# Column sums, roots of three columns and a predicted sum for the renewed x in the norms of a diffusion trunk step

## What is computed

```
h = modulate(x, norm_pre[0], m0, m1);  y = swiglu(h, gate, up, down)
x = x + 0.5 * m2 * rmsnorm(y, norm_post[0])
h = modulate(x, norm_pre[1], m3, m4);  y = token_mixer(h)     # three mixers, then w_out
x = x + m5 * rmsnorm(y, norm_post[1])
h = modulate(x, norm_pre[2], m6, m7);  y = swiglu(h, ...)
x = x + 0.5 * m8 * rmsnorm(y, norm_post[2])
modulate(x, g, shift, scale) = rmsnorm(x, g) * (1 + scale) + shift,   rmsnorm(x, g) = x / sqrt(mean(x^2) + eps) * g
m0..m8 = silu(cond) @ ada_w + ada_b, one set for context, one for latent tokens
```

## Time and profile before

| | us |
|---|---|
| median of 3 runs | 2229.18 (2228.59 to 2231.0) |
| profiled execution, from first to last instruction | 2228.5 |
| PE busy in it | 2145.9 |
| DVE, ACT, POOL busy | 915.8, 903.4, 1240.8 |
| DMA | 311.37 MB, mean 140 GB/s |

### The profile page before, as it was taken

The page is one execution under the profiler, slowest core; times in us unless marked ns, Lnnn a source line. Parts: engine busy times, 40 slices in busy tenths (PEclk is TensorE's granted clock), DMA queues, the critical chain, the costliest instruction groups (busy, mean ns, idle before and its releaser), DMA issues.

```text
span 2228.5 us, 32128 instructions
## 1 busy us (share of the span) xinstructions
PE 2145.9 (96%) x13212; PEld 2022.6 (91%) x13212; DVE 915.8 (41%) x1486; ACT 903.4 (41%) x1269; POOL 1240.8 (56%) x972
## 2 busy tenths in 40 slices
PE   6999999999899999999999999999999899899998
PEld 4999997988898988999979999799888899799997
DVE  5122116446766465121251221534576664622122
ACT  3222323246765534223243232324567546432332
POOL 2666553444478464666646666354435955366663
PEclk8999999999999999999999999999999999899999
DMA  7555674433222384445554446552322235244431
GB/s 282 160 163 172 224 237 162 124 88 95 67 86 86 109 297 117 129 133 171 193 185 124 138 124 234 194 152 87 87 78 76 86 114 176 61 136 128 124 123 67
DMA packets 306921, 311.37 MB, mean 140 GB/s; under 512 B 9923, under 2 KB 285655, under 8 KB 306775
## 3 DMA queue, kind: packets, MB, share of 16 engines
q1 hardware_dynamic: 299671, 303.55, 43.4%
q10 hardware_dynamic: 7104, 5.77, 0.8%
HBM read 305.35 MB, written 3.93 MB: 139 GB/s over the span
## 4 chain that ended last, share of the span: by engine, by line
PE 73%; DVE 12%; ACT 8%; POOL 3%; issue 2%; DMA 1%; SPq 0%; DVEq 0%; ACTq 0%
PE X L588 56%; PE S L588 6%; PE Ab L588 4%; POOL w_lo L525 2%; PE S L705 1%; ACT w_hi L1028 1%; POOL dec L553 1%; POOL dec L552 1%; PE X L766 1%; PE S L795 1%; ACT p L1181 1%; DVE mg_lo L1453 1%; DVE gate_b L1464 1%; PE X L848 1%; DVE root L1560 1%
## 5 line engine op out<-in xcount | busy, mean ns | idle before, releaser
L525 POOL TENSOR_TENSOR w_lo<-raw,w_hi 128x512 fp32r<-128x512 f32 (+1 forms) x872 | 1163.6, 1356 | 947.2 <-ACT w_hi L1028 938.2
L1028 ACT ACTIVATE w_hi<-raw 128x1024 fp32r<-128x1024 f32 (+1 forms) x436 | 453.3, 1041 | 723.6 <-PE X L588 687.7
L588 PE MATMUL X<-h_hi,w_hi 128*128 128x384 f32 x1600 | 539.7, 337 | 12.6 <-DVE h_lo L1518 12.6
L588 PE MATMUL X<-h_lo,w_hi 128*128 128x384 f32 x1600 | 536.8, 335 | 0.0
L588 PE MATMUL X<-h_hi,w_lo 128*128 128x384 f32 x1600 | 536.6, 335 | 0.0
L588 PEld LDWEIGHTS X<-h_hi,w_hi 128*128 128x128 f32 x1600 | 302.0, 189 | 24.5 <-DVE h_lo L1518 15.9
L588 PEld LDWEIGHTS X<-h_lo,w_hi 128*128 128x128 f32 x1600 | 302.0, 189 | 0.0
L588 PEld LDWEIGHTS X<-h_hi,w_lo 128*128 128x128 f32 x1600 | 301.9, 189 | 0.0
L1590 DVE TENSOR_TENSOR prod<-X,silu 128x768 f32<-128x768 f32 x44 | 42.1, 957 | 566.7 <-PE X L588 566.7
L588 PE MATMUL X<-act_hi,w_hi 128*128 128x384 f32 x704 | 236.4, 336 | 0.0
L588 PE MATMUL X<-act_hi,w_lo 128*128 128x384 f32 x704 | 235.3, 334 | 0.0
(11 more groups left out here) (364 smaller groups left out, 3075.3 us busy)
## 6 DMA issues: line engine op xcount, KB each, us to landing
raw<-in_w_in SPq DMA_DIRECT2D x124, 512.0 KB, 3.8
raw<-in_ffn_gate SPq DMA_DIRECT2D x88, 512.0 KB, 3.8
raw<-in_ffn_up SPq DMA_DIRECT2D x88, 512.0 KB, 3.7
raw<-in_ffn_down SPq DMA_DIRECT2D x80, 512.0 KB, 3.5
raw<-in_ada_w SPq DMA_DIRECT2D x48, 512.0 KB, 3.9
hold<-in_ada_w SPq DMA_DIRECT2D x29, 512.0 KB, 5.2
first_w<-in_ada_w SPq DMA_DIRECT2D x16, 512.0 KB, 10.6
hold_a<-in_ada_w SPq DMA_DIRECT2D x16, 512.0 KB, 6.4
```

The costliest lines, as they stand in the source:

```text
L525: ins = nc.gpsimd.tensor_tensor(slot(w_lo, u)[:, part], raw_of(u)[:, part], slot(w_hi, u)[:, part], SUB)
L588: mm = nc.tensor.matmul(dst, w[:, k, m * 128:m * 128 + 128], r_, start=start and k + j == 0, stop=stop and k == u.nk - 1 and j == 2)
L1028: A(slot(w_hi, u), raw_of(u), ACT.Copy).then_inc(hi_ready[u.split], 1)
```

## The change

Sums over D are made by matmuls that have the tile of squares as the stationary operand and a column of `pick` (three columns wide, a single one filled) as the moving one (`token_sums`): the sum of token p of block b lands in partition p, column b of a 128x3 tile. ACT takes the root of the 128x3 tile (`r_q`), DVE its reciprocal (`r_t`), and `spread` brings it back to 128 x 384: the column, broadcast to 128 columns, is stationary and the identity moves. The result stays in PSUM (`SPREAD`, banks S6 and S5).

The sum of squares of the new x isn't made from x. With g = gate * y and r the reciprocal root of y, it is the old sum + 2r * sum(x*g) + r^2 * sum(g*g) (`x_sum`, `grown`; `grown` is kept from going below minus the old sum). For that DVE makes g tile by tile (`gated`), x*g (`with_x`), adds both kinds of squares (`added`), and ACT squares y and g, a tile at a time (`squared`, `gated_squared`). The last pair is taken in two halves: PE signals its first tile with `half_done`.

`post` and `pre` become `joint`: x is renewed a tile at a time between the small steps, and the last five tiles between the scaled tiles; `SPREAD[1]` is read by them from PSUM. S6 is no longer a bank of `MOD`, which has two now, and the take of the gap's first group moves into `joint`, behind the scaled tile of k = 3; it was behind all of `pre`. PE's ada units are split 2, 3 and the rest. ACT's last `highs` of a y phase moves from behind the squares of the last pair into `gap`. In an `out` phase the factors of the next norm are made at pair 0 instead of 3. `first_pre` uses the short sums, too; `last_post` gets its factor spread, and `r_tok` from `r_q` directly. POOL's loop keeps its order. `first_in` semaphores are merged into `loaded`.

```diff
-        MOD = [Ab, S7, S6]
+        MOD = [Ab, S7]
+        SPREAD = (S6[:, 0:T], S5[:, 0:T])
...
-                if u.first and g >= 3:
-                    pe.wait_ge(S["ada_copied"], g - 2)
+                if u.first and g >= 2:
+                    pe.wait_ge(S["ada_copied"], g - 1)
...
+            def token_sums(dst, rows, start, stop):
+                for b, r in enumerate(tokens(rows)):
+                    mm = nc.tensor.matmul(dst[:, 0:NB], r, pick[:, NB - 1 - b:2 * NB - 1 - b], start=start and b == 0,
+                                          stop=stop and b == NB - 1)
+                return mm
+            def spread(dst, col):
+                for b in range(NB):
+                    mm = nc.tensor.matmul(dst[:, b * 128:b * 128 + 128], col[:, b:b + 1].broadcast_to([128, 128]), ident,
+                                          start=True, stop=True)
+                mm.then_inc(S["spread_ready"], 1)
+            def y_sums():
+                pe.wait_ge(S["parts_ready"], seen.next("parts_ready"))
+                token_sums(S5, silu[:, 0, :], True, False)
+                pe.wait_ge(S["y_sq_ready"], seen.next("y_sq_ready", KT) - 1)
+                token_sums(S5, prod[:, 0, :], False, False)
+                pe.wait_ge(S["y_sq_ready"], seen.value("y_sq_ready"))
+                token_sums(S5, prod[:, 2, :], False, True).then_inc(S["sum_ready"], 1)
             def gap(units):
                 y_sums()
-                early = 12 if len(units) > 12 else len(units) // 2
-                for u in units[:early]:
+                for u in units[:2]:
                     ada_unit(u)
-                x_sums([])
-                for u in units[early:]:
+                pe.wait_ge(S["r_ready"], seen.next("r_ready"))
+                spread(SPREAD[0], r_t)
+                pe.wait_ge(x_free[0], seen.value(("xf", 0)) + 1)
+                pe.wait_ge(S["parts_ready"], seen.next("parts_ready"))
+                token_sums(X[0][:, 0, 0:NB], y_sum, True, False)
+                pe.wait_ge(S["c_made"], seen.next("c_made", KT) - 1)
+                token_sums(X[0][:, 1, 0:NB], silu[:, 1, :], True, False)
+                token_sums(X[0][:, 1, 0:NB], prod[:, 1, :], False, False)
+                pe.wait_ge(S["parts_ready"], seen.next("parts_ready"))
+                token_sums(X[0][:, 0, 0:NB], part, False, True)
+                pe.wait_ge(S["c_made"], seen.value("c_made"))
+                token_sums(X[0][:, 1, 0:NB], prod[:, 3, :], False, True).then_inc(S["cross_ready"], 1)
+                for u in units[2:5]:
+                    ada_unit(u)
+                pe.wait_ge(S["r_ready"], seen.next("r_ready"))
+                spread(SPREAD[1], r_t)
+                for u in units[5:]:
                     ada_unit(u)
                 return by_tiles
...
             def x_sums(units):
                 for k in range(KT):
                     pe.wait_ge(S["x_sq_ready"], seen.next("x_sq_ready"))
-                    mm = nc.tensor.matmul(S5[:, 0:T], ones, sq[:, k, :], start=k == 0, stop=k == KT - 1)
+                    mm = token_sums(S5, sq[:, k, :], k == 0, k == KT - 1)
                     if k % 2 and k // 2 < len(units):
                         ada_unit(units[k // 2])
                 mm.then_inc(S["sum_ready"], 1)
+                pe.wait_ge(S["r_ready"], seen.next("r_ready"))
...
-                            act.wait_ge(unit_done[u.split], u.split_turn + 1)
                             outputs[u.tag[0]](u)
-                        highs(u.n + SPLIT + 1)
+                        if u.tag != ("y", 3) or not u.last:
+                            highs(u.n + SPLIT + 1)
...
-            def gap(units):
-                root_of_sums()
-                act.wait_ge(S["ada_used"], units[2].n + 1)
-                x_squares(0, KT)
-                root_of_sums()
+            def root_of_sums(sums):
+                A(r_q[:, :], sums, ACT.Sqrt, bias=eps[:, 0:1], scale=1.0 / D).then_inc(S["root_ready"], 1)
+            def gap(units, upto):
+                highs(upto)
+                act.wait_ge(S["x_sum_made"], seen.next("x_sum_made"))
+                root_of_sums(x_sum[:, :])
                 act.wait_ge(S["ada_used"], units[:9][-1].n + 1)
                 h_highs(0, KT)
...
+            def y_squares(halves_done, cross):
+                def squared(u, k):
+                    if k >= 3:
+                        act.wait_ge(S["y_added"], seen.next("y_added"))
+                    A(prod[:, k % 2 * 2, :] if k else silu[:, 0, :], X[u.dest][:, k % 2, 0:T], ACT.Square).then_inc(S["y_sq_ready"], 1)
+                def gated_squared(k):
+                    act.wait_ge(S["g_made"], seen.next("g_made"))
+                    A(prod[:, k % 2 * 2 + 1, :] if k else silu[:, 1, :], y[:, k, :], ACT.Square).then_inc(S["c_made"], 1)
+                def go(u):
+                    i = u.tag[1]
+                    if i < 3:
+                        act.wait_ge(unit_done[u.split], u.split_turn + 1)
+                        for k in (2 * i, 2 * i + 1):
+                            squared(u, k)
+                        for k in (2 * i, 2 * i + 1):
+                            if cross:
+                                gated_squared(k)
+                        return
+                    act.wait_ge(S["half_done"], halves_done)
+                    squared(u, 6)
+                    if cross:
+                        gated_squared(6)
+                    act.wait_ge(unit_done[u.split], u.split_turn + 1)
+                    squared(u, 7)
+                    act.wait_ge(S["sum_ready"], seen.next("sum_ready"))
+                    root_of_sums(S5[:, 0:NB])
+                    if cross:
+                        gated_squared(7)
+                return go
...
+            def inverse_root():
+                dve.wait_ge(S["root_ready"], seen.next("root_ready"))
+                V.reciprocal(r_t[:, :], r_q[:, :]).then_inc(S["r_ready"], 1)
+                dve.wait_ge(S["r_ready"], seen.next("r_ready"))
...
+            def joint(units):
+                def add_to_x(k):
+                    step(V.tensor_tensor(y[:, k, :], y[:, k, :], SPREAD[0], MUL))
+                    step(V.tensor_tensor(x[:, k, :], x[:, k, :], y[:, k, :], ADD))
+                inverse_root()
+                dve.wait_ge(S["spread_ready"], seen.next("spread_ready"))
+                add_to_x(0)
+                dve.wait_ge(S["cross_ready"], seen.next("cross_ready"))
+                step(V.tensor_tensor(grown[:, :], X[0][:, 1, 0:NB], r_t[:, :], MUL))
+                step(V.scalar_tensor_tensor(grown[:, :], X[0][:, 0, 0:NB], 2.0, grown[:, :], MUL, ADD))
+                step(V.tensor_tensor(grown[:, :], grown[:, :], r_t[:, :], MUL))
+                step(V.scalar_tensor_tensor(grown[:, :], x_sum[:, :], -1.0, grown[:, :], MUL, ALU.max))
+                V.tensor_tensor(x_sum[:, :], x_sum[:, :], grown[:, :], ADD).then_inc(S["x_sum_made"], 1)
+                add_to_x(1)
+                inverse_root()
+                add_to_x(2)
+                dve.wait_ge(S["spread_ready"], seen.next("spread_ready"))
+                dve.wait_ge(S["ada_used"], units[2].n + 1)
+                for k in range(KT):
+                    for g, (t0, t1) in GROUPS:
+                        ins = V.scalar_tensor_tensor(sq[:, k, t0:t1], x[:, k, t0:t1], mA[:, k, g:g + 1], SPREAD[1][:, t0:t1], MUL, MUL)
+                    ins.then_inc(S["norm_ready"], 1)
+                    if k == 3:
+                        ada_take(units[7])
+                    if k:
+                        low(k - 1)
+                    if k + 3 < KT:
+                        add_to_x(k + 3)
+                    dve.wait_ge(S["norm_ready"], seen.next("my_norm"))
+                low(KT - 1)
...
+            def y_out(cross):
+                def gated(u, k):
+                    dve.wait_ge(S["y_sq_ready"], KT * seen.value("y_phases") + k + 1)
+                    for g, (t0, t1) in GROUPS:
+                        ins = V.tensor_scalar(y[:, k, t0:t1], X[u.dest][:, k % 2, t0:t1], mG[:, k, g:g + 1], None, MUL)
+                    ins.then_inc(S["g_made"], 1)
+                    seen.next("g_made")
+                def with_x(k):
+                    if not cross:
+                        return
+                    dve.wait_ge(S["g_made"], KT * seen.value("y_phases") + k + 1)
+                    if k == 0:
+                        V.tensor_tensor(y_sum[:, :], x[:, k, :], y[:, k, :], MUL)
+                    elif k < KT - 1:
+                        step(V.tensor_tensor(part[:, :], x[:, k, :], y[:, k, :], MUL))
+                        step(V.tensor_tensor(y_sum[:, :], y_sum[:, :], part[:, :], ADD))
                     else:
-                        for k in (2 * c, 2 * c + 1):
-                            V.tensor_tensor(x[:, k, :], x[:, k, :], y[:, k, :], ADD).then_inc(S["x_ready"], 1)
-                    if c == 0:
-                        dve.wait_ge(S["tok_ready"], 1)
```

(46 more changed lines are left out.)

165 lines of the change are left out of this document (73 added, 92 removed).

## The result

The changed kernel takes 2276.56 us (median of four runs: 2257.7, 2276.4, 2276.7, 2276.9) against 2228.94 for the kernel before: a ratio of 1.0196, 95% interval 1.0175 to 1.0218. The prediction said 2238.9 with a range up to 2251. The direction was right, the size wrong by a factor of five.

A forecast was written before the change was run, and what follows sets the result against it. PE bounds the kernel, so only gaps in its weight streaming count. Losses 11.1 + 5.5 less gains 4.5, 1.5 and 0.9 make 9.7 us lost on a span of 2228.5: 2238.9 as a run, range 2224 to 2251.

The forecast's parts named there:

- part 1: In the gaps: reciprocals 0.16 instead of 2.56 us, roots 0.2 instead of 0.59, each short sum 0.67, bounds 0.33 and 0.67.
- part 2: Chain of the gaps after a down phase: each loses 3.7 us with the clock's cost, three of them 11.1.
- The two-bank wait: PE waits 3.8 us at unit 16 for DVE's transpose; head starts at T0+22.8 instead of 20.9, 1.8 lost.
- The clock's charge: In each 22-unit gap the clock falls around the bank wait, costing 2.0 us, bounds 0 and 2.5.
- Part 3: Gaps after an out phase: layer 0 loses 5.5 us; layer 1, without a bank wait, gains 4.5.
- Part 4: Start and end of the kernel: 1.5 us gained at the start, 0.9 at the end.
- Holds and narrow sums are cheap: Rival: the clock stays full and a short sum in the gaps costs 0.33 us; 2225.3 us, chance 0.15.
- The clock holds: Rival: the clock does not fall at the gaps' PE waits of 3.8 us; 2230.8 us, chance 0.2.
- The clock falls early: Rival: clock falls in PE's idle 3.2 us after out; 4.7 more in two gaps, 1 in others; 2251, chance 0.15.
- slower: Outcome for the whole kernel: a time above 2233.6 us, chance 0.62.
- same: Outcome for the whole kernel: a time from 2224.7 to 2233.6 us, chance 0.28.
- faster: Outcome for the whole kernel: a time below 2224.7 us, chance 0.10.

The follow-up runs named there:

- e2: The changed kernel with 128 instead of 3 columns moved in each short sum; 2243.5 us, ratio 1.0071.
- a0: The changed kernel run again unedited, beside the kernel before on the same chip; 2271.4 us, ratio 1.0195.
- e1: The changed kernel with the transpose of units[7] moved from behind the fourth scaled tile to behind the first; 2239.1 us, ratio 1.0046.
- e4: The kernel before with only the three-column sums, small roots and reciprocals, and spreads added, three banks kept; 2246.1 us, ratio 1.0062.
- e6: The kernel before with only short sums, small roots and spreads added, each short sum moving 128 columns; 2219.2 us, ratio 0.9946.
- e3: The kernel before with only two modulation banks and the transpose of units[7] inside the scaling loop at k == 3; 2256.1 us, ratio 1.0130.
- e5: The changed kernel with the transpose of units[7] after the first scaled tile and 128 columns in the short sums; 2220.2 us, ratio 0.9953.

## Why the prediction was wrong, step by step

**The step that failed: "I take 0.112 ... 0.67 per sum, bounds 0.33 and 0.67" (part 1).** The value was right at the full clock: six passes in 0.67, so of the two figures that the prediction set beside its own, 0.64 and 0.15 a sum, the first is borne out. The bound above it was not right. I took 0.67 as the dear end and never asked what such passes do to the granted clock. At half clock a sum took 1.14 to 1.29, so 0.67 was the cheap end in this kernel. That one bound carries into part 2 (first scaled tile at 16.6 for 12.1), the start, and the range.

**What the forecast describes is e2.** With the sums dense, the first gap follows the prediction's list: the reciprocal ended at T0+4.3 (4.2), the second at 11.0 (10.9), the first scaled tile started at 12.2 (12.1), the transpose ended at 20.1 (20.2), the bank wait was 3.45 (3.8), the head started at 23.0 (22.8). The head ends of e2 against before give +2.1, +5.2, +3.5, +4.9 and -4.0, together 11.7; predicted were 3.7, 5.5, 3.7, 3.7 and -4.5, together 12.1. a0 lies 32.5 us above the forecast, and the wider sums take 28 of them away (2271.4 less 2243.5): that is the clock lost under and between the short sums, nearly all of it before the bank wait. e2's own profile is 14.1 us longer than before's: 11.7 in the gaps, -0.6 before the first T0, -0.1 at the end, and 3.1 in the stretches between, where I had set nothing.

**The two-bank wait (part 2): held.** Place, releaser, length and the 2.7 us to the head's start are in the trace of after. Its worth I understated: without it the changed kernel was 32 us faster, and the wait's own length is 13.8 of that; some 8.5 are the falls of the clock in or behind it in three gaps, and some 10 are clock that e1 lost less elsewhere, which stays open (e1). Put alone into the old kernel it cost 29.

**The clock's charge (part 2): near in size, not in every gap.** I charged 2.0 a gap for a fall around the bank wait. In e2, where only that wait is left, the gaps after a down phase ended at 39.8, 41.1 and 42.5: the first had full clock throughout, the others lost 1.3 and 2.8 against it, 1.4 in the mean of three. But I had asked of every *wait* whether the clock would fall in it, because the four falls of the earlier trace rows were waits. I never asked it of *work*.
The Trainium skill, TensorE: Matmul & The Clock Gate, "HAM oscillation — how this bites in real kernels", tells of idle time between matmuls as what sends the clock down. By that rule alone e4 and e6, with nearly the same waits in that gap, would have the same clock; the rows show 0.50 and 1.00. The falls inside the waits of e3 (6.24 us, clock 0.50) agree with it; and in the shorter run of the changed kernel a wait of 3.46 (363.3 to 366.8) passed with the clock full. So idle time is one thing that precedes a fall here, and it doesn't tell e4 from e6.

**Part 3.** Layer 0: +5.5 predicted; +5.5 in the first profile of after, +10.2 in a0, +5.2 in e2. DVE came to k=6 at T0+2.1 (838.24) as I counted (2.3). The agreement of the first profile is partly luck, since it holds some lost clock. Layer 1: -4.5 predicted, +0.7 measured; in e2 and e5, with the clock held in the sums, -4.0 and -4.8. The chain of work was right, the clock took the gain. (The prediction has the old head end there at 41.3; it is 41.9.)

**Part 4.** At the start I forecast 1.5 won; after lost 3.6. The x sums there are of three columns too. The stretch over them, after, then e2:

```profile
20.40:30.40 10.00, 9.44 (x58) 7.38 (x61) 0.98 (x4) 1.53 (x3) 0.57 (x1) 0.50 1.05 391
```

```profile
20.40:30.40 10.00, 7.14 (x86) 4.92 (x78) 4.05 (x15) 1.45 (x3) 0.49 (x1) 1.00 1.05 391
```

Half clock against full. The first modulation tile then comes at 29.71 instead of 26.44, just as POOL starts (29.83, for 4.96), and four instructions of 16 columns take 0.94 to 1.19 beside it, of which one row:

```profile
32.41 1.19 DVE L1552 TENSOR_SCALAR mA<-mA 128x16 f32<-128x16 f32 x1
```

It took 0.17 in e2, where the four are done before POOL starts. So a clock lost on PE came back as DVE instructions slowed beside POOL. In e2 the first T0 is 0.6 earlier than before: of the 1.5 forecast, 0.6 is there. The end gave 0.2 of the forecast 0.9.

**The rivals.** "Holds and narrow sums are cheap" is dead: 0.112 a pass. "The clock holds" (0.2, 2230.8) is out too: it held through the bank wait in some gaps, but not in the sums. "The clock falls early" (0.15, 2251) was nearest, with the wrong cause and a third of the extra loss: I let it fall in an idle 3.2 us after `out`, for two spreads and five sums, and gave 1 us to each of the three other gaps. It fell in all five gaps and at the start, 2 to 5 us behind T0, at or behind the short sums of y, and stayed low under all or some of the cross sums.

**The chances.** I gave 0.62 to slower, which was right in sign, and a range that had no case above 2251. (By its own parts "same" adds up to 0.305 and "faster" to 0.075, not 0.28 and 0.10.) A case in which the new short matmuls lower the clock wherever they stand could have been priced from the same terms: eight sums and two spreads of 0.67 a gap at half speed are 6.7 us more, in five gaps 33, so 2272. This is an estimate in hindsight, and that it lands so near is partly luck: most of the sums of y were over when the clock fell, and a sum at half clock took 1.14 to 1.29, not 1.34.

## What to carry to other kernels

When a change replaces large matmuls by short ones on the path, price them at both levels of TensorE's clock, and read the granted clock of the stretch beside its busy share; a stretch can be busy for 100% and still be at 0.50. Where a short matmul takes as long with more moving columns, try it with more: here 128 cost the same 0.67 us a sum as 3 and gave 27 us back. A double buffer that "covers" only a wait can be worth more than that wait: count what is queued behind it, and move the release earlier before giving the buffer up.

## What was not expected of the hardware

- Fp32 passes with a 128x128 stationary operand cost 0.112 us whether 3 or 128 columns move (six in 0.67). At half clock three columns cost 0.19 to 0.22 a pass.
- The granted clock fell from 1.00 to 0.50 in the middle of 48 such passes with no hole between them (e4), and didn't with 128 columns (e6). What exactly the chip counts is left open: only these two widths were run, and the added columns were mostly ones, so width and content changed together.
- The same kernel ran at anything from 2257.7 to 2278.3 us, with falls in the same part of each gap but of different number and length. Where a path hangs on the clock, one profile is not enough: after `out` of layer 0 the first profile of after shows a loss of 5.5 us and that of a0 one of 10.2 (head end 43.1 and 47.9).
- A wait alone lowers it as well: in e3 it fell to 0.50 inside idle waits of 6.24 us, while waits of 3.46 in the changed kernel had a fall in or behind them in some gaps and not in others.
